# A two-layer encoder kernel: residual stream held feature-major, 1/rms applied behind the projections, layers unrolled

## What is computed

```python
def rms_norm(x, g):
    return x * lax.rsqrt(jnp.mean(x * x, axis=-1, keepdims=True) + EPS) * g

h = x
for l in range(DEPTH):                                  # DEPTH = 2
    h = h + hybrid_mixer(rms_norm(h, mix_norm_g[l]), w_in[l], ...)   # mLSTM | neighbourhood attention | GLA
    h = h + memory_cross_attention(rms_norm(h, xattn_norm_g[l]),
                                   rms_norm(mem, mem_norm_g[l]), w_xq[l], w_xk[l], w_xv[l], w_xo[l])
    h = h + conv_ffn(rms_norm(h, ffn_norm_g[l]), w_up[l], ffn_conv_w[l], ffn_conv_b[l], w_down[l])
return rms_norm(h, final_norm_g)

def conv_ffn(h, w_up, conv_w, conv_b, w_down):
    u = h @ w_up
    a, g = u[..., :D_FF], u[..., D_FF:]
    return (gelu(dwconv_centred(a, conv_w, conv_b)) * g) @ w_down   # conv over tokens, width 3
```

## Time and profile before

| | us |
|---|---|
| median of 3 runs | 986.36 (985.79 to 993.02) |
| span of the profiled execution | 984.5 |
| PE busy | 946.2 |
| DVE busy | 577.6 |
| ACT busy | 495.7 |
| POOL busy | 11.6 |

### The profile page before, as it was taken

How to read it: one execution, slowest core, us unless ns; L and a number is a source line. 1 busy time by engine, 2 the same in 40 slices (tenths; PEclk the granted TensorE clock), 3 DMA queues, 4 the chain that set the end, 5 groups by cost and what they waited for, 6 DMA issues and landing times.

```text
span 984.5 us, 17146 instructions
## 1 busy us (share of the span) xinstructions
PE 946.2 (96%) x6492; PEld 858.4 (87%) x6492; DVE 577.6 (59%) x771; ACT 495.7 (50%) x692; POOL 11.6 (1%) x39
## 2 busy tenths in 40 slices
PE   4999999999999999999989999999999999999997
PEld 4998889788888999999879998897888799999996
DVE  2796566466437655656457764674554475565654
ACT  4854674246446444444467347433465374444443
POOL 4000000000000000000000000000000000000000
PEclk9999999999999999999989999999999999999999
DMA  7934533233425556555446443532452355655541
GB/s 184 255 109 120 181 129 129 87 128 130 170 69 171 190 171 205 181 177 179 121 128 171 111 136 129 172 129 86 128 172 85 129 171 172 213 171 182 186 168 43
DMA packets 128416, 146.98 MB, mean 149 GB/s; under 512 B 23132, under 2 KB 109514, under 8 KB 128330
## 3 DMA queue, kind: packets, MB, share of 16 engines
q1 hardware_dynamic: 128042, 144.78, 46.1%
q10 hardware_dynamic: 288, 1.05, 0.3%
HBM read 144.77 MB, written 1.05 MB: 148 GB/s over the span
## 4 chain that ended last, share of the span: by engine, by line
PE 91%; DVE 3%; issue 2%; ACT 2%; SPq 1%; DMA 0%; DVEq 0%; ACTq 0%
PE bank L549 26%; PE bank L550 25%; PE bank L551 25%; PE bank L604 2%; PE bank L675 1%; PE bank L810 1%; PE bank L795 1%; PE bank L709 1%; PE bank L708 1%; PE bank L771 1%; PE bank L697 1%; SPq L446 1%; PE bank L766 1%; ACT xhi L895 1%; PE bank L663 1%
## 5 line engine op out<-in xcount | busy, mean ns | idle before, releaser
L1120 DVE TENSOR_TENSOR wlo<-raw,whi 128x2048 fp32r<-128x2048 f32 (+3 forms) x144 | 306.9, 2135 | 195.4 <-ACT whi L887 195.0
L549 PE MATMUL bank<-xhi,whi 128*128 128x256 f32 x1184 | 339.9, 287 | 2.3 <-DVE xlo L1140 2.0
L550 PE MATMUL bank<-xlo,whi 128*128 128x256 f32 x1184 | 336.1, 284 | 0.0
L551 PE MATMUL bank<-xhi,wlo 128*128 128x256 f32 x1184 | 335.8, 284 | 0.0
L887 ACT ACTIVATE whi<-raw 128x2048 fp32r<-128x2048 f32 (+3 forms) x144 | 256.7, 1788 | 48.1 <-PE bank L551 43.7
L549 PEld LDWEIGHTS bank<-xhi,whi 128*128 128x128 f32 x1184 | 227.8, 192 | 8.0 <-DVE xlo L1140 3.4
L550 PEld LDWEIGHTS bank<-xlo,whi 128*128 128x128 f32 x1184 | 228.0, 193 | 0.8
L551 PEld LDWEIGHTS bank<-xhi,wlo 128*128 128x128 f32 x1184 | 228.0, 193 | 0.0
L549 PE MATMUL bank<-whi,xhi 128*128 128x512 f32 (+2 forms) x352 | 128.0, 364 | 1.2 <-DVE xlo L1140 1.2
L550 PE MATMUL bank<-wlo,xhi 128*128 128x512 f32 (+2 forms) x352 | 126.0, 358 | 0.0
L551 PE MATMUL bank<-whi,xlo 128*128 128x512 f32 (+2 forms) x352 | 126.0, 358 | 0.0
(11 more groups left out here) (221 smaller groups left out, 911.7 us busy)
## 6 DMA issues: line engine op xcount, KB each, us to landing
raw<-in_w_up SPq DMA_DIRECT2D x44, 1024.0 KB, 5.1
raw<-in_w_down SPq DMA_DIRECT2D x22, 1024.0 KB, 4.9
raw<-in_w_in SPq DMA_DIRECT2D x10, 1024.0 KB, 6.4
raw<-in_w_xk SPq DMA_DIRECT2D x8, 1024.0 KB, 5.0
raw<-in_w_xv SPq DMA_DIRECT2D x8, 1024.0 KB, 5.0
raw<-in_w_out SPq DMA_DIRECT2D x8, 1024.0 KB, 5.1
raw<-in_w_xq SPq DMA_DIRECT2D x8, 1024.0 KB, 6.0
raw<-in_w_xo SPq DMA_DIRECT2D x8, 1024.0 KB, 4.9
```

The lines of the kernel that those rows point to most:

```text
L549: mm(o, s_hi, m_hi, start=first, stop=False, skip_group_check=True)
L550: mm(o, s_hi, m_lo, start=False, stop=False, skip_group_check=True)
L551: return mm(o, s_lo, m_hi, start=False, stop=last, skip_group_check=True)
L1120: tt(wlo[:, u % RING, 0:n], raw[:, u % RING, 0:n], whi[:, u % RING, 0:n], ALU.subtract).then_inc(lo_done, 1)
```

## The change

- **Residual feature-major.** `hT` (features x tokens) takes the place of `h`. `w_out` and `w_xo` are fetched and multiplied in the form of `fm_unit`, and `w_down` of layer 0 too; `w_down` of layer 1 stays token-major. x is transposed once at the start (plain float32 transposes), and `hT` once back in layer 1 (ht, 16 transposes behind the first `fg`).
- **Norms behind the product.** `take_in` adds a bank into `hT` (DVE), scales by the gain and rounds (ACT), squares (ACT) and forms the low part (DVE); the product then runs on the unnormed activations. POOL adds up the squares, PE sums them over the partitions (`square_sums`, r1 to r3: one float32 matmul of 256 columns and two of 2 columns), ACT takes the root, DVE the reciprocal of 128 x 260 values (`inverse_root`). Each bank of a projection is multiplied by it as it is drained. Where the factor lies along tokens in the free dimension DVE does this: mix, nqk4, qk0 to qk2 (into `araw`), nq, nk, gq, gk, xq, fa (into `fraw`), fg (into `fgs`). Six turns (n1 to n3) and the diagonals go.
- **Memory** is normed and transposed in layer 0 only and kept as `memT`; each layer applies its gain.
- **Layers unrolled**, units numbered through (144), the first two units of layer 1 split before layer 0 ends.
- **Parameters** of layer 0 come on the ACT queue, those of layer 1 during layer 0 (behind unit 8 on SP), transposed behind kt1.

Seven pieces, in this order: the form of the `w_out` units; POOL's sums of squares; PE's list at the start of a layer; PE's list at the cross-attention; ACT's `take_in`, its first gate operations and its taps in the q/k stage; DVE's `take_in`, `inverse_root`, its first gate operations and its part of the q/k stage; and the end of layer 0 on DVE, which ACT has too.

```diff
-    u += tm("w_out", 0, 512) + tm("w_out", 512, 512)
+    u += [fm("w_out", (256 * i, 256)) for i in range(4)]
...
+            for i in range(3 * DEPTH):
+                for c in range(1, 4):
+                    pool.wait_ge(sq_ready, 4 * i + c + 1)
+                    step(g.tensor_tensor(sqs[:, 0, :], sqs[:, 0, :], sqs[:, c, :], ALU.add))
+                g.tensor_tensor(sqs[:, 0, 0:T], sqs[:, 0, 0:T], sqs[:, 0, T:2 * T], ALU.add).then_inc(acc_ready, 1)
...
-                turn("n1", h, 1, parameters)
+                if l == 0:
+                    turn("x", xtm, lambda i: pe.wait_ge(tok_in[i // 2], 16))
+                    pe.wait_ge(const_ready, 2)
+                    parameters("par", 0)
                 fm_unit(0, "mix", "n1")
+                square_sums(1)
                 fm_unit(1, "nqk4")
...
-                turn("n2", h, 6)
                 for i in range(4):
-                    fm_unit(U_XQ + i, f"xq{i}", None if i else "n2")
+                    fm_unit(U_XQ + i, f"xq{i}", None if i else "n2", (yhi, ylo))
+                    if i == 0:
+                        square_sums(2)
...
+            def take_in(l, names, dst, lg, gcol, u=None):
+                for i in range(4):
+                    if u is not None:
+                        hi_upto(l * U + u + i + 3)
+                    is_drained(act, l, names[i])
+                    scaled_hi(dst, hT, lg, gcol, i)
+                    squares(i)
...
                 split_hi(3)
+                root_of_mean(l, 1)
                 act.wait_ge(const_ready, 2)
-                act.wait_ge(gate_in, layer_base(0, 16 * 3, l, 16 * 3))
-                is_filled(act, l, "mix")
+                act.wait_ge(gate_in, 16 * 3 * (l + 1))
+                is_drained(act, l, "mix")
...
                 for i in range(3):
                     split_hi(5 + i)
-                    is_filled(act, l, f"qk{i}")
+                    is_drained(act, l, f"qk{i}")
                     for f in range(2):
                         j = 2 * i + f
-                        last = A(qk[:, j, :], bank(f"qk{i}", 2, T)[:, f, :], ACT.Identity,
+                        last = A(qk[:, j, :], araw[:, i % 2, f, :], ACT.Identity,
...
+            def take_in(l, names, dst, hi, lx, group, gcol, u=None):
+                for i in range(4):
+                    if u is not None:
+                        lo_upto(l * U + u + i + 3)
+                    if i:
+                        scaled_lo(dst, hi, hT, lx, lx, group, gcol, i - 1)
+                    is_filled(dve, l, names[i])
+                    hh = hT[:, 2 * i:2 * i + 2, :]
+                    tt(hh, hh, bank(names[i], 2, T), ALU.add).then_inc(drained["D"], 1)
+                scaled_lo(dst, hi, hT, lx, lx, group, gcol, 3)
+
+            def inverse_root(l, i):
+                is_drained(dve, l, f"r{i}")
+                link(V.reciprocal(rs[:, 0:T + 4], rs[:, 0:T + 4]))
+                ts(rs[:, T + 4:T + 8], rs[:, T:T + 4], 0.5, None, ALU.mult).then_inc(rs_ready, 1)
+                dve.wait_ge(rs_ready, 3 * l + i)
...
                 split_lo(3)
                 dve.wait_ge(const_ready, 2)
+                inverse_root(l, 1)
+                is_filled(dve, l, "mix")
+                drain(tt(mixs[:, :], bank("mix")[:, 0:T], rs[:, 0:T], ALU.mult))
                 split_lo(4)
...
                 for i in range(3):
                     split_lo(5 + i)
-                    dve.wait_ge(conv_ready, layer_base(0, 3, l, i + 1))
+                    is_filled(dve, l, f"qk{i}")
+                    b = araw[:, i % 2]
+                    drain(tt(b, bank(f"qk{i}", 2, T), across, ALU.mult))
+                    dve.wait_ge(conv_ready, 3 * l + i + 1)
...
+                if l + 1 < DEPTH:
+                    split_lo(U + 2)
+                    take_in(l, [f"fd{i}" for i in range(4)], xlo, xhi, l + 1, "n1", R_MIX)
```

More of the change, by code:

```diff
@@ new lines, in parameters, with square_sums @@
+                def parameters(name, at):
+                    pe.wait_ge(prm_in, 16 * NPRM * (at + 1))
+                    free(name)
+                    nc.tensor.transpose(bank(name)[:, 0:RA], rowa[:, :], ident[0:RA, 0:RA])
+                    nc.tensor.transpose(bank(name)[:, P:P + RB], rowb[:, :], ident[0:RB, 0:RB]).then_inc(te_done, 1)
+                def square_sums(i):
+                    name = f"r{i}"
+                    free(name)
+                    pe.wait_ge(acc_ready, 3 * l + i)
+                    acc = sqs[:, 0, 0:T]
+                    mm(bank(name)[:, 0:T], ones[:, 0:P], acc, start=True, stop=True)
+                    for t in range(TT):
+                        last = mm(bank(name)[:, T + 2 * t:T + 2 * t + 2], acc[:, t * P:(t + 1) * P], ones[:, 0:2], start=True, stop=True)
+                    last.then_inc(te_done, 1)
@@ L890, in turned, with root_of_mean @@
+            def root_of_mean(l, i):
+                is_filled(act, l, f"r{i}")
+                A(rs[:, 0:T + 4], bank(f"r{i}")[:, 0:T + 4], ACT.Sqrt, scale=1.0 / DM, bias=eps[:, :]).then_inc(drained["A"], 1)
+            for l in range(DEPTH):
+                pcol = pcols[:, l, :]
+                def split_hi(upto):
+                    hi_upto(l * U + upto)
                 def turned(group, gcol, n=4):
@@ L935, in _ @@
+                if l == 0:
+                    for i in range(4):
+                        is_drained(act, l, f"x_{i}")
+                        squares(i)
+                    table(ACT.Sqrt)
+                    is_drained(act, l, "par")
+                    for i in range(4):
+                        scaled_hi(xhi, hT, l, R_MIX, i)
                 split_hi(3)
+                root_of_mean(l, 1)
                 act.wait_ge(const_ready, 2)
-                act.wait_ge(gate_in, layer_base(0, 16 * 3, l, 16 * 3))
@@ L1142, in turned @@
                         drain(last)
-                def residual(name, u):
-                    for n in range(2):
-                        for t in range(TT):
-                            split_lo(u + min(2 * n + t + 3, 5))
-                            is_filled(dve, l, f"{name}{n}_{t}")
-                            hh = h[:, t, n * 512:(n + 1) * 512]
-                            last = tt(hh, hh, bank(f"{name}{n}_{t}"), ALU.add)
-                            drain(last)
-                    is_drained(dve, l, f"{name}1_1")
@@ L1160, in _ @@
+                if l == 0:
+                    for i in range(4):
+                        is_filled(dve, l, f"x_{i}")
+                        drain(V.tensor_copy(hT[:, 2 * i:2 * i + 2, :], bank(f"x_{i}", 2, T)))
+                    parameters("par", 0)
+                    for i in range(4):
+                        scaled_lo(xlo, xhi, hT, l, l, "n1", R_MIX, i)
                 split_lo(3)
                 dve.wait_ge(const_ready, 2)
+                inverse_root(l, 1)
+                is_filled(dve, l, "mix")
```

716 lines of the change are left out of this document (381 added, 335 removed).

## The result

The changed kernel takes 1019.9 us (median of 4 runs, 1017.6 to 1022.5) where the kernel before takes 986.1: a ratio of 1.034, with a 95% interval from 1.030 to 1.038. That is 34 us slower. The forecast was 999.7, with 976 to 1009 as its range. So the side was right, and the size was not: the range was missed by 11 us.

What follows compares the result with a forecast made beforehand. PE was taken to bound the kernel, busy 946.2 of 984.5 us. Terms 7.2 - 5.2 - 2.9 + 6.8 + 1.6 + 1.0 + 4.8 sum to +13.3: span 997.8, time 999.7 us, range 976 to 1009.

Steps and rivals of the forecast that it cites:

- the chains: The forecast itself: slower through chains of DVE and ACT that PE waits for, 994 to 1004 us, chance 0.38.
- The step on `take_in`: From `w_out` to xq: adds 7.0 us a bank where PE needs 5.8; costs 4.9 for 5.4 before, -0.6.
- the term for the clock: At the start, PE stands ahead of `par` and `mix`; one slow stretch charged, +1.6 us.
- +1.0 at the boundary: End of layer 0 to layer 1: new stalls of about 4 us may lower the clock again, +1.0 us.
- -1.4 for the one that goes: At the layer boundary, the low clock behind the old turn goes, -1.4 us.
- could bring a slow stretch of about 1.4: Clock rival: new stalls at transitions and q/k stages add +3 to +8 us; POOL or clock on top, chance 0.16.
- the memory in layer 0: Memory turn of layer 0: 16 transposes take its place, with 0.4 left for waits between banks, -1.5 us.
- the heads: mLSTM heads: three DVE drains ahead of the weights and a late nq split, +2.4 us a layer, +4.8 in all.
- `w_down`: Eleven `w_down` units of layer 0 take longer as products in the new form, +2.2 us.
- The rest of the FFN: Costed at nothing: DVE's work rises from 10.0 to 11.4 of 17.09 us a step, and PE covers it.
- The start: `mix` starts as before, 21.8 for 21.72; PE then stands 1.6 us before the gates; 0.1 charged for the start.
- The POOL rival: POOL's sums hold up DVE's low parts at six places, +6 to +9 us; POOL or clock on top, chance 0.16.

Runs made afterwards that it cites:

- take2: The changed kernel with `take_in` reordered on ACT and DVE, each bank followed by the split of the weight unit whose slot it frees: 994.7 us, ratio 1.009.
- the idle matmuls: The changed kernel with matmuls whose results are thrown away ahead of PE's waits, none at the start (second form): 1007.1 us, ratio 1.021.
- the kernel of all together: The changed kernel with the new orders in `take_in` and the q/k stage, parameters transposed without waiting for POOL's constants: 984.5 us, ratio 0.998.
- early: The changed kernel with parameters transposed without waiting for POOL's constants and unit 0 split ahead of the high and low parts: 1012.3 us, ratio 1.029.

## Why the prediction was right and wrong

**Right, the chains.** The place and the period were as written: DVE's adds in `w_out` stand 6.98 us apart for 7.0 worked out, the heads start 36.1 us behind the gates for 34.3 (some 1.6 of it slow clock), and the reciprocal takes 1.78 us for 1.75:

```profile
28.83 1.78 DVE L1218 RECIPROCAL rs<-rs 128x260 f32<-128x260 f32 x1 [2.48 <-ACT rs L963]
```

The step on `take_in` (-0.6, with 0.8 for the product: +0.2) fits n2 once the slow clock is taken off: 4.9 - 4.3 over two layers. That it fits to 0.1 us is luck, as the count is not that good. `take2` showed that this loop was the cause, and that it lay in the order alone.

**Wrong, the term for the clock.** The step that failed reads "I charge one slow stretch: +1.6", with +1.0 at the boundary and -1.4 for the one that goes. Measured, there are eleven stretches of 1.1 to 2.5 us, 21.1 in all, less 2.9 before: +18.2 where the sum has +1.2. By this count that is 17 of the 18 us missed in the span; the idle matmuls gave back 13.6. The prediction had this as a rival, that each of the new stalls "could bring a slow stretch of about 1.4", and gave it 0.16 together with POOL. It was no rival but in the main a consequence: the sum itself contained stalls of 2 to 4 us at most of these places, and the earlier trace rows already showed what PE does behind a longer one. That 2 to 3 us are enough no row of before showed: in that kernel PE's four waits of 1.4 us ahead of the turns n2 and n3 have no slow stretch behind them. The Trainium skill ("TensorE: Matmul & The Clock Gate", on how the clock's oscillation bites in real kernels) tells of a kernel that pays for the slow clock again at every wait; this trace agrees in that, at nine places behind waits of 1 to 3 us, but not at every wait: those ahead of the second v unit have none. The price per place was low too: 1.4 us came from a stretch of 3.2 us, and at n3 or the heads it lasted 6.8 us.

**Wrong, the memory in layer 0.** The term was -1.5, and the stage has +3.5. Of the 5.0 us between them 2.0 are slow clock. The rest is a wait of 3.1 us for the first low part: ACT copies all four banks into `memT` before it rounds the first, where before it took them from the bank. The rows of ACT and PE:

```profile
146.77 2.10 ACT L1082 ACTIVATE memT<-bank 128x512 f32<-128x512 f32 x4
150.87 0.55 PE L589 MATMUL bank<-xhi,whi 128*128 128x256 f32 x1 [3.12 <-DVE xlo L1202]
```

The change puts four copies on the path, and I had counted only PE's part of the turn.

**Too dear: the heads.** 2.4 a layer were forecast for drains ahead of the weights of each head, and 3.6 measured, of which 2.5 are slow clock. So the drains cost 1.1: 0.5 of it is a wait for the split of the nq unit, and PE waited 0.23 and 0.53 for DVE's weights in the third and fourth head where it waited 0.31 and 0.20.

**Too dear: `w_down`.** +2.2 was forecast for eleven units in the other form. A step takes 17.09 us as before, and in layer 1, where the form did not change, 16.85. The `w_down` unit in the new form takes 5.70 us for 5.59, so +0.1 and not +0.2, and the 96 matmuls of a step take 11.4 and 11.3 us now and 11.5 before; the cause of that was not looked for. The rest of the FFN was right: DVE works 11.6 of 17.09 us a step, and no step is longer than before.

**The start.** The first product came at 23.1, not 21.8. POOL's additions slow the low parts by 2.0 us, and without them it comes at 21.2. PE's wait of 6.0 us for POOL's constants is not the cause: in the kernel of all together the parameters no longer wait for them, and the first product is only 0.24 us earlier. The POOL rival held here, and at n2 and n3 it did not. PE then stood 1.7 us ahead of the gates, for 1.6. The sum left out one term here: r1's own matmuls take 0.8 us of PE between `mix` and `nqk4`.

## What to carry to other kernels

A stall on PE is priced with what it does to the clock behind it: here most stalls of 2 to 3 us cost 1.3 to 2.5 us more, and a change that replaces few long waits by many short ones pays it many times. Before such a change is given up, the queues of the helping engines are put in the order of need: what PE waits for next goes ahead of the split of weights that it needs two units later. That gave back 25 us in `take_in` alone and 35 with the q/k stage, with the same operations, and only then did idle matmuls in the remaining stalls bring the kernel below the old one. A fair rival to it was not built: the kernel before with idle matmuls at the end of layer 0 alone, where they took 1.9 us off the stage.

## What the runs showed of the hardware

Three things I had not expected. An idle matmul is worth its place only if the wait behind it is real: 20 of them cost 1.9 us where the wait was 0.5 us, and gave 1.4 to 2.4 us where there was a real one. When stalls go, slow stretches can turn up elsewhere, as at 187 to 197 in two kernels (4.7 us) and in the first 70 us of `early`. And a stage can take one of two times with the same instructions: nine steps of the FFN of layer 0 take 153.8 us in seven kernels and 152.1 in seven others, and the attention takes 17.7 or 19.4, the latter with a slow stretch of some 3.4 us in it. So a change at one place is read from several stages or from a median, not from one.
